# The softmax factors of a windowed attention, moved from VectorE to ScalarE

## The chip, the cores and the metric

The kernel runs on one core of one Trainium2 chip. The metric is the device time of the whole program in microseconds (us), median of several runs. The engines named below are TensorE (PE in the profile; its weight loads are PEld), VectorE (DVE), ScalarE (ACT), GpSimd (POOL) and SyncE (SP, which issues most DMAs).

## The reference, cut to what matters

The program computes two stacked transformer blocks: attention with a sink and a window, an MLP, a gated scan, a second MLP, and then a second model with attention, a state space layer and a mixture of experts. The change touches only the first attention, of 512 latent and 256 context tokens, with 16 heads of 64 in 4 groups that share keys:

```
def softmax_with_sink(s, sink):
    sk = sink.astype(jnp.float32)[None, :, :, None, None]
    m = jnp.maximum(jnp.max(s, axis=-1, keepdims=True), sk)
    e = jnp.exp(s - m)
    return e / (jnp.sum(e, axis=-1, keepdims=True) + jnp.exp(sk - m))
...
        p = softmax_with_sink(jnp.concatenate([s_lat, s_ctx], axis=-1), sink_g).astype(v.dtype)
        return (jnp.einsum('bhgqk,bkhd->bqhgd', p[..., :n_loc], v)
                + jnp.einsum('bhgqk,bkhd->bqhgd', p[..., n_loc:], v_ctx))
```

The kernel divides after the product with the values: it needs 1/(sum of the exponentials and the sink's term) for each query, which this text calls the factors.

## The kernel before, in words

All weights stream through a ring of four buffers. Each engine's program is written out by hand, in order, and semaphores tie the engines together; no planner reorders anything. So an instruction that waits holds up all that stands behind it on its engine.

The attention is 24 blocks (`WORK`, line 1019), numbered n: 4 groups of heads times 6 blocks of 128 queries, taken in the order b = 0, 1, 4, 2, 3, 5. Blocks 0 to 3 are latent and see their own key tile, the neighbours' and the two context tiles; blocks 4 and 5 are context and see the two context tiles alone. So the blocks of a group have 4, 5, 2, 5, 4 and 2 key tiles ("four-key", "five-key", "two-key" blocks below), 88 in all. Each key tile has 512 columns: 4 heads times 128 queries.

For block n TensorE does this in order (lines 1234 to 1248): for each key tile `key_scores` (lines 1209, 1212 and, at the window's edge, 1214) into one of two PSUM banks XP 0 and 1, where tile s waits until the exponential of tile s-2 has been taken; `turn_rows(n+1)` (line 1200), which waits for the sink's term of block n+1; a product that opens the output bank (line 1243); and for each key tile `weighted_values` (line 1221, each recorded as two products), which waits for the exponential of its tile. Among these stand the four `row_scores` of block n+2 (lines 1188 to 1194), whose first waits for `rows_low(n+1)` and whose third and fourth wait for VectorE's maxima of the first and second. VF holds ones beside the values, so rows 64 to 127 of the output bank (XP 2 + n % 2) are the sums, each of them in all 64 rows.

ScalarE for block n (line 1858 on): the exponential of each key tile (`exps`, line 1849), after the first of them `sink_term(n+1)` (line 1828); then `rows_high(n+1)` (1833), `queries_high(n+1)` (1841), and `mixed_high(n-1)` (1853), which waits for the divided output of block n-1.

VectorE for block n (line 2566 on): `normalise(n-1)`, `rows_low(n+1)` (line 2536), `mixed_low(n-1)` (line 2558), which waits for `mixed_high(n-1)`, and `maxima(n+2)` (four reductions in line 2521, then small steps in lines 2524 to 2531). `normalise` takes the factors in three steps, a transposition in 32 by 32 squares out of PSUM (line 2543), the reciprocal of the one column of each square that is needed (line 2545) and a transposition back of that column spread out (line 2547), and then multiplies the two halves of the output by them (line 2552).

After the last block come `normalise(23)`, `mixed_high(23)` and `mixed_low(23)`, and only then can TensorE begin the product with w_o (line 645).

Of the kernel before, what the change touches and what calls it, by code (L numbers as in the profile page):

```python
# [19 lines left out]
ACT = mybir.ActivationFunctionType  # L20
AX = mybir.AxisListType

P = 128
# [197 lines left out]
def backbone_kernel(nc, a, out_d):  # L221
# [19 lines left out]
    with ctx:  # L241
        sem_cache = {}

        def sem(name):
            if name not in sem_cache:
                sem_cache[name] = ctx.enter_context(nc.semaphore(name))
            return sem_cache[name]

        def sb(stack, name, shape, dt=F32):
            return stack.enter_context(nc.sbuf_tensor(name, shape, dt))  # L250
# [4 lines left out]
        with ExitStack() as s0:  # L255
            PT = sb(s0, "PT", [P, PT_RING, 512])
            QB = sb(s0, "QB", [P, 2, 4, P], FR)
            SPREAD = sb(s0, "SPREAD", [P, 4, P])
            RC = sb(s0, "RC", [P, 2, 2, P])
            RCT = sb(s0, "RCT", [64, 512])  # L260
            RCS = sb(s0, "RCS", [64, 16])
            OU = sb(s0, "OU", [P, 2, 2, P])

        with ExitStack() as s7:
# [280 lines left out]
        XP = ctx.enter_context(nc.psum_tensor("XP", [P, 4, 512], F32))  # L545
# [72 lines left out]
        def pieces(it, t, tokens):  # L618

            if it == 0 and t < 2:  # L620
                return [(2 * t + c, c, *halves_of(tokens)[t][0:2]) for c in range(2)]
            if tokens == T:
                return [(2 * t + c, t, 384 * c, 384 * c + 384) for c in range(2)]
            return [(t + 2, t, 0, LAT)]
# [396 lines left out]
        def values_through(n):  # L1021

            return WORK[n][5] + len(WORK[n][4])
# [702 lines left out]
        def _(act):  # L1726
# [98 lines left out]
            def sink_term(n):  # L1825

                act.wait_ge(sem("shift_spread"), 2 * n + 2)
                act.activation(SPREAD[:, :, 68:72], SINKS[:, :, :], ACT.Exp).then_inc(sem("sink_term"), 1)

            def rows_high(n):  # L1830

                act.wait_ge(sem("rows_turned"), n + 1)
                act.activation(QB[64:96, n % 2, :, :].rearrange("p (x c) n -> p x (c n)", x=2), DP[64:96, 1:4:2, 256:512], ACT.Copy
                               ).then_inc(sem("rows_high"), 1)

            def queries_high(n, g, b):

                if n >= 2:
                    act.wait_ge(sem("attended"), values_through(n - 2))
                for e in range(2):  # L1840
                    act.activation(QB[0:64, n % 2, 2 * e:2 * e + 2, :], A2[64 * e:64 * e + 64, e, 2 * g:2 * g + 2, b * P:(b + 1) * P].bitcast(F32),
                                   ACT.Copy).then_inc(sem("queries_copied"), 1)

            def exps(s):

                act.wait_ge(sem("keyed"), s + 1)
                if s >= PT_RING:
                    act.wait_ge(sem("attended"), s - PT_RING + 1)
                act.activation(PT[:, s % PT_RING, :], XP[:, s % 2, :], ACT.Exp).then_inc(sem("exponentials"), 1)

            def mixed_high(n, g, b):
                act.wait_ge(sem("normalised"), 2 * n + 2)
                act.activation(AH[:, 2 * g:2 * g + 2, b * P:(b + 1) * P], OU[:, n % 2, :, :], ACT.Copy).then_inc(sem("mixed_high"), 1)

            sink_term(0)
            rows_high(0)
            queries_high(0, 0, 0)
            for n, g, b, near, keys, first in WORK:
                for i in range(len(keys)):
                    exps(first + i)  # L1860
                    if i == 0 and n + 1 < len(WORK):
                        sink_term(n + 1)
                if n + 1 < len(WORK):
                    rows_high(n + 1)
                    queries_high(*WORK[n + 1][0:3])
                if n:
                    mixed_high(*WORK[n - 1][0:3])
            mixed_high(n, g, b)
            at.u += 32
            split_high(act, at, nxt)  # L1870
# [435 lines left out]
            for t in range(2):  # L2306
                split_high(act, at, nxt)
                for jj in range(2):
                    j = 2 * t + jj
# [93 lines left out]
        def _(dve):  # L2403
# [133 lines left out]

            def normalise(n):

                dve.wait_ge(sem("attended"), values_through(n))  # L2540
                bank_of = 2 + n % 2
                turned = RCT[:, :].rearrange("p (b n) -> p b n", n=32)
                dve.transpose(RCT[:, :], XP[64:P, bank_of, :]).then_inc(sem("denominators"), 1)
                dve.wait_ge(sem("denominators"), 3 * n + 1)
                dve.reciprocal(RCS[:, :], turned[:, :, 0:1].rearrange("p b n -> p (b n)")).then_inc(sem("denominators"), 1)
                dve.wait_ge(sem("denominators"), 3 * n + 2)
                dve.transpose(RC[0:64, :, :, :].rearrange("p e j n -> p (e j n)").rearrange("p (b n) -> p b n", n=32),
                              RCS[:, :].unsqueeze(2).to_broadcast((64, 16, 32))).then_inc(sem("denominators"), 1)
                dve.wait_ge(sem("denominators"), 3 * n + 3)
                out = XP[0:64, bank_of, :].rearrange("p (e j n) -> p e j n", e=2, j=2)  # L2550
                for e in range(2):
                    dve.tensor_tensor(OU[64 * e:64 * e + 64, n % 2, :, :], out[:, e, :, :], RC[0:64, e, :, :], ALU.mult
                                      ).then_inc(sem("normalised"), 1)
# [12 lines left out]
            for n, g, b, near, keys, first in WORK:  # L2566
                if n:
                    normalise(n - 1)
                if n + 1 < len(WORK):
                    rows_low(n + 1)  # L2570
                if n:
                    mixed_low(*WORK[n - 1][0:3])
                if n + 2 < len(WORK):
                    maxima(*WORK[n + 2][0:4])
            normalise(n)
            mixed_low(n, g, b)
            split_low(dve, nxt)
# [43 lines left out]
            for it in range(MLP_STEPS):  # L2621
# [14 lines left out]
                for t in range(2 * KT):  # L2636
# [5 lines left out]
                    for c in range(2):  # L2642
                        i = 2 * t + c
# [6 lines left out]
                        if t < KT:  # L2650
                            if i >= 2:
                                dve.wait_ge(sem("hidden_high"), it * 16 + (i - 1))
                            n = pieces(it, t, T)[c][3] - pieces(it, t, T)[c][2]
# [490 lines left out]
            for t in range(2):  # L3144
                split_low(dve, nxt)
                for jj in range(2):
                    j = 2 * t + jj
# [303 lines left out]
```

## Time and profile before

| what | us |
|---|---|
| median of 3 runs | 2658.0 (2656.53 to 2661.26) |
| the profiled execution | 2659.49 |
| its span | 2656.7 |
| TensorE busy in the span | 2461.1 |
| VectorE busy | 1693.7 |
| ScalarE busy | 1088.6 |

The profiled execution took 2.8 us more than its span, and 1.5 us more than the median. The attention's blocks run from about 206 to 409 us from the span's start. Shapes in rows are partitions by elements, and durations of single instructions include their latency, so neighbours on one engine may overlap a little.

### The profile page before, as it was taken

Reading aid. Unit: us, or ns where it says so; the run is one execution under the profiler, and the core shown is the slowest. Engines: PE = TensorE matmul, PEld = TensorE weight load, DVE = VectorE, ACT = ScalarE, POOL = GpSimd, SP = SyncE. Lnnn points to the kernel's source line nnn. Section 1 sums busy time; section 2 is a strip of 40 time slices with the busy share of each in tenths; the row PEclk is TensorE's granted clock in tenths of the full one; section 3 lists DMA queues with packets and bytes.
Section 4 is the critical chain, followed back from the end, with each engine's and each line's share of the span. In section 5 each row is a group of like instructions: output and inputs, shape, how many; then the busy total and the mean of one; then the engine's idle time right before and its main releaser. Section 6 shows DMA issues by size and latency. Waiting matters only on the chain. (4 is left out here: it accounts for less than half of the span.)

```text
span 2656.7 us, 32750 instructions
## 1 busy us (share of the span) xinstructions
PE 2461.1 (93%) x12252; PEld 2036.7 (77%) x12252; DVE 1693.7 (64%) x2746; ACT 1088.6 (41%) x1739; POOL 94.3 (4%) x111
## 2 busy tenths in 40 slices
PE   6968899899999999899998899998989999999999
PEld 5865558699999997687777688886766666777777
DVE  6666778765646466655553634445347997569986
ACT  4424443431313133423333422333446663377764
POOL 0000000000000000000000000000000330020000
PEclk8989999899999999889999999998999999999999
DMA  6220004133323232011111122222121221149995
GB/s 255 84 91 0 1 1 159 51 133 127 127 96 127 103 127 82 22 48 48 40 40 48 63 97 96 101 91 94 64 72 44 72 71 64 49 164 341 338 336 183
DMA packets 78131, 275.62 MB, mean 104 GB/s; under 512 B 8800, under 2 KB 9312, under 8 KB 77856
## 3 DMA queue, kind: packets, MB, share of 16 engines
q1 hardware_dynamic: 74016, 265.74, 28.5%
q10 hardware_dynamic: 3968, 7.88, 0.9%
q8 instruction: 97, 1.59, 0.2%
q14 instruction: 50, 0.41, 0.0%
HBM read 271.49 MB, written 2.10 MB: 103 GB/s over the span
## 5 line engine op out<-in xcount | busy, mean ns | idle before, releaser
L645 PE MATMUL DP<-HH,WL 128*128 128x384 f32 (+2 forms) x1408 | 517.7, 368 | 28.3 <-DVE WL L638 22.5
L646 PE MATMUL DP<-HH,WH 128*128 128x384 f32 (+2 forms) x1408 | 504.6, 358 | 0.0
L647 PE MATMUL DP<-HL,WH 128*128 128x384 f32 (+2 forms) x1408 | 504.5, 358 | 0.0
L638 DVE TENSOR_TENSOR WL<-RAW,WH 128x1024 fp32r<-128x1024 f32 x230 | 280.8, 1223 | 218.7 <-ACT WH L611 212.0
L645 PE MATMUL DP<-A,WL 128*128 128x384 f32 (+2 forms) x1072 | 381.7, 356 | 22.6 <-issue 8.4
L646 PE MATMUL DP<-A,WH 128*128 128x384 f32 (+2 forms) x1072 | 379.1, 354 | 0.0
L647 PE MATMUL DP<-A,WH 128*128 128x384 f32 (+2 forms) x1072 | 378.8, 353 | 0.0
L611 ACT ACTIVATE WH<-RAW 128x1024 fp32r<-128x1024 f32 x230 | 241.2, 1050 | 292.6 <-PE DP L647 205.0
L645 PEld LDWEIGHTS DP<-HH,WL 128*128 128x128 f32 x1408 | 267.5, 190 | 66.8 <-DVE WL L638 31.8
L646 PEld LDWEIGHTS DP<-HH,WH 128*128 128x128 f32 x1408 | 267.6, 190 | 29.2 <-issue 5.2
L647 PEld LDWEIGHTS DP<-HL,WH 128*128 128x128 f32 x1408 | 267.3, 190 | 25.5
L645 PEld LDWEIGHTS DP<-A,WL 128*128 128x128 f32 x1072 | 204.0, 190 | 43.1 <-issue 14.7
L775 DVE SCALAR_TENSOR_TENSOR MPROD<-RAW,COND 128x1024 f32<-128x1024 f32 x180 | 219.9, 1222 | 14.4 <-DMA RAW<-in_stream 7.1
L646 PEld LDWEIGHTS DP<-A,WH 128*128 128x128 f32 x1072 | 204.1, 190 | 16.6 <-issue 0.5
L647 PEld LDWEIGHTS DP<-A,WH 128*128 128x128 f32 x1072 | 204.0, 190 | 16.4
L3298 DVE TENSOR_TENSOR MW<-MRAW,MW 128x1024 fp32r<-128x1024 f32 x168 | 196.3, 1229 | 18.1 <-ACT MW L2352 17.8
L2352 ACT ACTIVATE MW<-MRAW 128x1024 fp32r<-128x1024 f32 x168 | 163.9, 1052 | 0.0
L645 PE MATMUL DP<-WH,HL 128*128 128x256 f32 x304 | 94.7, 311 | 18.5 <-issue 17.6
L2633 DVE TENSOR_TENSOR Y<-DP,Y 128x384 f32<-128x384 f32 (+2 forms) x64 | 35.1, 554 | 111.7 <-PE DP L647 111.7
L1920 ACT ACTIVATE SQ<-TQ 128x384 f32<-128x384 f32 (+2 forms) x64 | 33.6, 525 | 162.8 <-DVE TQ L2654 162.8
L645 PE MATMUL DP<-MW,G 128*128 128x512 f32 x224 | 89.4, 399 | 7.0 <-DVE MW L3298 6.9
L646 PE MATMUL DP<-WH,HH 128*128 128x256 f32 x304 | 92.0, 303 | 0.0
(419 smaller groups left out, 3863.7 us busy)
## 6 DMA issues: line engine op xcount, KB each, us to landing
RAW<-in_stream SPq DMA_DIRECT2D x326, 512.0 KB, 3.3
MRAW<-in_stream SPq DMA_DIRECT2D x168, 512.0 KB, 5.4
MATS<-in_ssm ACTq DMA_DIRECT2D x16, 256.0 KB, 2.6
X<-in_x SPq DMA_DIRECT2D x8, 384.0 KB, 10.0
BW<-in_rel ACTq DMA_DIRECT2D x4, 512.0 KB, 3.5
out<-X SPq DMA_DIRECT2D x8, 256.0 KB, 2.0
COND<-in_cond SPq DMA_DIRECT2D x1, 1024.0 KB, 4.9
CONST<-in_const SPq DMA_DIRECT2D x1, 256.0 KB, 4.9
```

The costliest lines, as they stand in the source:

```text
L611: act.activation(WH[:, nxt.d % WRING, :], RAW[:, nxt.u % RING, :], ACT.Copy).then_inc(hi_done, 1)
L638: dve.tensor_tensor(WL[:, w, :], RAW[:, nxt.u % RING, :], WH[:, w, :].bitcast(F32), ALU.subtract).then_inc(raw_done[nxt.u % RING], 1)
L645: pe.matmul(out, al, bh, start=first, stop=False)
L646: pe.matmul(out, ah, bh, start=False, stop=False)
L647: return pe.matmul(out, ah, bl, start=False, stop=last)
L775: dve.scalar_tensor_tensor(MPROD[:, :], RAW[:, at.u % RING, :], 1.0, COND[:, s, :], ALU.mult, ALU.mult, accum_out=MODT[:, col, s:s + 1]).t ...
L1920: act.activation(SQ[:, i % 2, 0:b0 - a0], r, ACT.Square)
L2352: act.activation(MW(i, 0)[:, t, :], MRAW[:, j % ERING, :], ACT.Copy).then_inc(hi_done, 1)
L2633: dve.tensor_tensor(y, DP[:, bank(at), 0:b0 - a0], y, ALU.add).then_inc(bank_free[bank(at)], 1)
L3298: dve.tensor_tensor(MW(i, 1)[:, t, :], MRAW[:, j % ERING, :], MW(i, 0)[:, t, :].bitcast(F32), ALU.subtract).then_inc(sem("expert_taken"), 1)
```

## The change

ScalarE makes the factors as exp(-ln(sum)), straight over the 64 rows of sums. A function `denominators(n-1)` with two activations is put into ScalarE's program of block n behind the first exponential and `sink_term(n+1)`, ahead of the second exponential; the one of the last block stands after the loop. VectorE's three steps and their buffers go, and `normalise` waits for ScalarE's two steps in their place.

```
             def mixed_high(n, g, b):
...
+            def denominators(n):
+
+                act.wait_ge(sem("attended"), values_through(n))
+                if n:
+                    act.wait_ge(sem("normalised"), 2 * n)
+                over = RC[0:64, :, :, :].rearrange("p e j n -> p (e j n)")
+                act.activation(over, XP[64:P, 2 + n % 2, :], ACT.Ln).then_inc(sem("denominators"), 1)
+                act.wait_ge(sem("denominators"), 2 * n + 1)
+                act.activation(over, over, ACT.Exp, scale=-1.0).then_inc(sem("denominators"), 1)
+
...
                     exps(first + i)
                     if i == 0 and n + 1 < len(WORK):
                         sink_term(n + 1)
+                    if i == 0 and n:
+                        denominators(n - 1)
...
                 if n:
                     mixed_high(*WORK[n - 1][0:3])
+            denominators(n)
             mixed_high(n, g, b)
...
             def normalise(n):
 
-                dve.wait_ge(sem("attended"), values_through(n))
                 bank_of = 2 + n % 2
-                turned = RCT[:, :].rearrange("p (b n) -> p b n", n=32)
-                dve.transpose(RCT[:, :], XP[64:P, bank_of, :]).then_inc(sem("denominators"), 1)
-                dve.wait_ge(sem("denominators"), 3 * n + 1)
-                dve.reciprocal(RCS[:, :], turned[:, :, 0:1].rearrange("p b n -> p (b n)")).then_inc(sem("denominators"), 1)
-                dve.wait_ge(sem("denominators"), 3 * n + 2)
-                dve.transpose(RC[0:64, :, :, :].rearrange("p e j n -> p (e j n)").rearrange("p (b n) -> p b n", n=32),
-                              RCS[:, :].unsqueeze(2).to_broadcast((64, 16, 32))).then_inc(sem("denominators"), 1)
-                dve.wait_ge(sem("denominators"), 3 * n + 3)
+                dve.wait_ge(sem("denominators"), 2 * n + 2)
```

## Rows read from the trace of the kernel before

**Rows 1.** Stretch: length, PE, PEld, DVE, ACT, POOL busy, granted clock, DMA share, GB/s.

```profile
206.00:409.00 203.00, 181.01 (x721) 109.25 (x720) 150.53 (x326) 95.39 (x205) 0.00 (x0) 1.00 0.00 1
225.00:233.00 8.00, 6.21 (x29) 3.90 (x28) 7.28 (x15) 3.13 (x7) 0.00 (x0) 1.00 0.01 3
```

**Rows 2.** Waits from 206 to 409: who waited for whom, total, times, longest.

```profile
PEld XP L1209 <- ACT PT L1849: 18.5, 32, 0.7
...
PE DP L1188 <- DVE QB L2536: 4.4, 7, 0.6
```

**Rows 3.** Groups by line, 206 to 412: busy, mean ns, idle before and its releaser.

```profile
L1849 ACT ACTIVATE PT<-XP 128x512 f32<-128x512 f32 x88 | 50.8, 593 | 99.1 <-PE XP L1212 54.8 <-PE XP L1214 44.3
...
L2543 DVE STREAM_TRANSPOSE RCT<-XP 64x512 f32<-64x512 f32 x24 | 17.2, 719 | 1.8 <-PE XP L1221 1.1
L2547 DVE STREAM_TRANSPOSE RC<-RCS 64x512 f32<-64x512 f32 x24 | 16.9, 703 | 0.8
...
L2545 DVE RECIPROCAL RCS<-RCT 64x16 f32<-64x16 f32 x24 | 5.9, 246 | 0.8
```

**Rows 4.** ScalarE's groups of the whole program, by shape.

```profile
L2170 ACT ACT_TABLE_LOAD x14 | 18.0, 1283 | 0.3
...
L2228 ACT ACTIVATE RS<-XP,EPSV 128x512 f32<-128x512 f32 x8 | 5.1, 692 | 8.9 <-PE XP L1525 8.9
...
L2232 ACT ACTIVATE RS<-RS 128x512 f32<-128x512 f32 x8 | 4.4, 620 | 0.0
```

**Rows 5.** Timeline of ScalarE outside the attention: start, duration, what.

```profile
49.68 0.90 ACT L855 ACTIVATE TR<-XP,EPSV 128x768 f32<-128x768 f32 x1
50.61 0.84 ACT L858 ACTIVATE TR<-TR 128x768 f32<-128x768 f32 x1
...
1115.50 0.62 ACT L1941 ACTIVATE QD<-BC 128x512 f32<-128x512 f32 x1
1116.02 0.62 ACT L1942 ACTIVATE KI<-BC 128x512 f32<-128x512 f32 x1
```

**Rows 6.** Timeline of a five-key block.

```profile
284.95 0.58 ACT L1849 ACTIVATE PT<-XP 128x512 f32<-128x512 f32 x1
...
285.77 0.39 PE L1209 MATMUL XP<-A,KDH 128*128 128x512 f32 x1
...
285.97 1.09 ACT L1849 ACTIVATE PT<-XP 128x512 f32<-128x512 f32 x2 [0.43 <-PE XP L1214]
...
286.62 0.50 PE L1209 MATMUL XP<-A,KDH 128*128 128x512 f32 x1 [0.23 <-ACT PT L1849]
```

**Rows 7.** Timeline of a four-key block.

```profile
294.11 0.59 ACT L1849 ACTIVATE PT<-XP 128x512 f32<-128x512 f32 x1
...
294.75 0.50 PE L1209 MATMUL XP<-A,KDH 128*128 128x512 f32 x1
```

**Rows 8.** Timeline of a two-key block.

```profile
277.49 0.72 DVE L2543 STREAM_TRANSPOSE RCT<-XP 64x512 f32<-64x512 f32 x1
...
277.61 0.58 ACT L1849 ACTIVATE PT<-XP 128x512 f32<-128x512 f32 x1
...
278.45 0.59 ACT L1833 ACTIVATE QB<-DP 32x512 fp32r<-32x512 f32 x1 [0.26 <-PE DP L1200]
...
279.26 0.87 DVE L2552 TENSOR_TENSOR OU<-XP,RC 64x256 f32<-64x256 f32 x2
280.16 0.69 DVE L2536 TENSOR_TENSOR QB<-DP,QB 32x512 fp32r<-32x512 f32 x1
...
281.00 0.35 PE L1188 MATMUL DP<-KDH,A 128*128 128x256 f32 x1 [0.63 <-DVE QB L2536]
...
281.62 2.69 DVE L2521 TENSOR_REDUCE TOP<-DP 128x1 f32<-128x512 f32 x4 [0.31 <-PE DP L1194]
```

**Rows 9.** Timeline of the last block.

```profile
403.82 0.19 PEld L1221 LDWEIGHTS XP<-PT,VF 128*128 128x128 f32 x1 [0.24 <-ACT PT L1849]
...
407.51 0.87 DVE L2552 TENSOR_TENSOR OU<-XP,RC 64x256 f32<-64x256 f32 x2
```

More of the change, by code:

```diff
@@ L259, in backbone_kernel @@
             RC = sb(s0, "RC", [P, 2, 2, P])
-            RCT = sb(s0, "RCT", [64, 512])
-            RCS = sb(s0, "RCS", [64, 16])
             OU = sb(s0, "OU", [P, 2, 2, P])
```

## The prediction

> **What bounds the kernel now.** I read the page's totals first: TensorE is busy 93% of the span, VectorE 64%, ScalarE 41%. That says nothing of the attention, so the second view is the busy time by stretch. In the 203 us of the 24 blocks TensorE is busy 181.0 us, VectorE 150.5, ScalarE 95.4, at a granted clock of 1.00 and without DMA traffic [rows 1]. TensorE is the fullest engine and has 22 us of gaps. The third view, the waits, says what ends them: most often a score product waits for an exponential (its weight load, 32 times, 18.5 us), and 7 times, in two-key blocks, the row scores wait for VectorE's `rows_low`, 4.4 us [rows 2]. ScalarE in turn idles 99 us ahead of exponentials [rows 3], but that idle time lies ahead of the first one of a block, while TensorE is at values and row scores. Within the key phase the two engines alternate over two PSUM banks, and there ScalarE has hardly a gap. The timelines of one block of each length [rows 6 to 8] show that, and on them the sum rests. The semaphores leave no other order: score tile s waits for exponential s-2.
>
> **What goes.** VectorE loses 24 transpositions of 719 ns, 24 reciprocals of 246 ns and 24 transpositions of 703 ns [rows 3], 40.0 us of busy time, and from the start of the first transposition to the first multiplication 279.26 - 277.49 = 1.77 us each time [rows 8]. What would be late next is the wait for ScalarE, worked out below.
>
> **What comes.** ScalarE gets 24 logarithms and 24 exponentials of 64x512. An exponential of 512 columns out of PSUM takes 0.58 to 0.60 us (593 ns mean) [rows 3, 6, 7], one from SBUF to SBUF 0.62 [rows 4, 5]. The only logarithms of 512 columns in the trace take 0.69 and read a bias from a tensor (EPSV) [rows 4]; the new one has none. So it costs between 0.58 and 0.69, and I take 0.60, by the exponential that also reads PSUM and has no bias operand. Half the partitions buy nothing: I keep the duration of 128, since no row of this shape speaks for less. The second must wait for the first; the same pair elsewhere shows 0.03 us between (49.68 + 0.90 = 50.58, then 50.61), and independent activations start 0.10 before the end of the one ahead (1115.50 + 0.62 against 1116.02) [rows 5]. The pair therefore moves the second exponential of a block by 0.60 + 0.03 + 0.62 - 0.10 = 1.15 us. Shortest: 1.10. Longest, with 0.69 and no overlap behind the pair: 1.34. The pair doesn't wait itself: the values of block n-1 are done before block n's keys, as TensorE goes in order, and so is `normalise(n-2)`. Queued behind it are the block's other exponentials, `rows_high`, `queries_high` and `mixed_high`.
>
> The Trainium skill ("ScalarE: Activation LUTs", section "What ACT_TABLE_LOAD costs") gives an activation with immediate scale and bias 186 ns + 0.833 ns per column, and some 93 ns more for each pointer operand; an estimate by it is 0.61 us for the logarithm, and the trace agrees in that the row with EPSV stands at 0.69. Were the bias handed over as a pointer after all, the pair would shift things by 1.24, and the sum below would be 14.4 in place of 13.1.
>
> **Five-key blocks (8).** The second exponential moves from 284.95 to 286.10 and ends at 286.68. The fourth score tile waits for it and starts 0.05 later, at 286.73 in place of 285.77 [rows 6]: 0.96 late. The third exponential follows in half a microsecond (two take 1.09), 286.60 to 287.19, where before it began at 285.97 because its scores weren't ready. So the fifth tile starts at 287.24 in place of 286.62: 0.62 late, a third of the shift being taken up by the gap of 0.43 that ScalarE had there. Nothing later in the block waits for slack: `turn_rows`, the values and the row scores follow in a chain on TensorE. 8 x 0.62 = 5.0. Bounds 0.57 and 0.80 (0.19 more with the longest pair): 4.6 and 6.4.
>
> **Four-key blocks (8, of which the first has no pair ahead).** The second exponential moves from 294.11 to 295.26 and ends at 295.85; the last score tile starts at 295.90 in place of 294.75 [rows 7], 1.15 late, with no gap behind it. 7 x 1.15 = 8.1; bounds 7.7 and 9.4.
>
> **Two-key blocks (7 without the last).** No score tile waits, but the second value product and the rest of ScalarE's queue do. From 277.61: logarithm to 278.21, exponential 278.24 to 278.86, the block's second exponential 278.76 to 279.34, `rows_high` from 279.26 in place of 278.45, to 279.85. VectorE multiplies from 278.90 (0.36 earlier than 279.26) to 279.77, so `rows_low` begins at 279.88 in place of 280.16, and the row scores at 280.72 in place of 281.00 [rows 8]: 0.28 early. TensorE's value products, moved by some 0.4, are still done by then, since it waited 0.63 there. But `queries_high` (0.85) and `mixed_high` (0.42) now end near 281.18 and `mixed_low` near 281.63, so the maxima start at 281.66, against 281.62: the gain is eaten, because the row scores wait for the maxima. In the other kind of two-key block, where the maxima began later, about 0.1 is kept. I take -0.2 for all 7; bounds -1.9 (0.28 each kept) and +1.1 (0.15 each, pair at its longest).
>
> **The end.** The second value product waits for the exponential that now comes 1.15 later [rows 9], and the last pair takes 1.25 with its start where the last transposition chain took 1.77, which had itself started half a microsecond after the values because of `mixed_low(22)`. The last multiplication then starts at 407.75 instead of 407.51: +0.2; bounds 0 and 0.5.
>
> **The sum.** 5.0 + 8.1 - 0.2 + 0.2 = 13.1 us; from the bounds 10.4 to 17.4. The profiled execution took 2659.5, so it becomes 2672.6. The median of the runs stood 1.5 below it at 2658.0, so I forecast a median of 2671.1 (2668.4 to 2675.4 by the bounds). Behind the attention all is moved as one: the weight ring stands full and no transfer runs [rows 1], so no stage after it gives time back. The 40 us that VectorE saves are worth nothing, as it then stands waiting for ScalarE.
>
> **The rivals.** *VectorE's chain sets the end, and ScalarE's pair hides in its idle time.* For it: ScalarE is idle more than half of the stretch, VectorE is at 7.28 of 8.00 us in a two-key block [rows 1], and the row scores wait for `rows_low`. Against it: the pair stands ahead of the second exponential by program order, and the idle time is elsewhere. It decides if ScalarE reaches the second exponential no later than TensorE needs it. Then the 4.4 us of waits [rows 2] go and 0.5 at the end: 2658.0 - 4.9 = 2653.1. Chance 0.05.
>
> *The stalls are partly made good*, because a later wait of the same block (for the maxima, the sink's term) was long enough to take them, so that only four-key blocks lose, about half: 2658 + 4 = 2662. Against it: those waits follow TensorE's own products by a fixed chain and move with them. Chance 0.07.
>
> *The pair costs more than its two durations*: the whole of ScalarE's tail comes late in two-key blocks as well, row scores start late in place of early, 0.5 each, and the pair is at its longest: 6.4 + 9.4 + 3.5 + 0.5 = 19.8, 2677.8. Chance 0.10.
>
> *Tables are switched.* If logarithm and exponential needed their own tables, 48 loads of 1283 ns [rows 4] would add 61.6 us: some 2733. Against it: the pair at 49.68 and 50.61 runs with no load between [rows 5]. The Trainium skill (same page, section "Table sets: the hidden batching unit") says that one set holds both functions; I found none of its loads within the attention. Chance 0.02. The forecast keeps 0.76.
>
> **How the numbers follow.** A difference under 0.2%, 5.3 us, can't be told from none here. Faster by more: nearly only the first rival's upper part, 0.04. Within: the rest of it and most of the second, 0.07. Slower: 0.89. The range for 8 in 10 takes in the bounds of the sum and reaches toward the second and third rivals: 2664 to 2679.
>
> **What would show it.** ScalarE's second exponential starts some 1.15 later after the first one in each block but block 0; the waits of L1209 for L1849 grow by some 13 us; the fourth tile of a five-key block and the last of a four-key block carry them; the multiplication starts 0.3 earlier in relation to the sink's term; the maxima in two-key blocks stay where they were; the attention's stretch takes 216 us, at clock 1.00, and no stage behind it changes its length. TensorE stood at 78% busy in 225 to 233 at a granted clock of 1.00 [rows 1], so 84% over the stretch should not lower it. A lower clock there, a table load, a logarithm over 0.7 us, or key phases that don't lengthen would prove the forecast wrong.

## The result, and the profile after

The changed kernel takes 2680.1 us in the median (2678.4 to 2686.3, 4 runs) against 2659.6 (2656.5 to 2662.2, 4 runs): ratio 1.0082, 95% interval 1.0067 to 1.0096. A second set of 5 runs gave 1.0083 (1.0069 to 1.0097). It is 20.5 us slower; the forecast had 13.1, and its range ended at 2679.0.

The busy time by stretch of the kernel after (columns as in [rows 1]), the attention's whole length. It begins 4.9 us later here, so the stretch is laid as in [rows 1], from 1.1 us ahead of the first exponential:

```profile
210.90:435.70 224.80, 186.52 (x721) 109.79 (x720) 110.47 (x254) 126.06 (x253) 0.00 (x0) 0.98 0.00 1
```

The stretch is 21.8 us longer. VectorE's busy time falls by 40 us and ScalarE's rises by 31, TensorE's work is the same 721 matmuls, and the mean clock is no longer 1.00: the granted clock is 0.50 up to 3.0 us behind the first exponential, and once more from 327.6 to 331.0 us. The waits of the same kernel, 211 to 436 us, answer to [rows 2]:

```profile
DVE OU L2555 <- ACT RC L1861: 40.3, 24, 3.5
...
PEld XP L1207 <- ACT PT L1847: 36.5, 39, 2.1
PE XP L1207 <- ACT PT L1847: 21.5, 27, 1.7
...
PE DP L1186 <- DVE QB L2547: 2.1, 7, 0.3
```

The loads of score products waited 18.5 us for exponentials before and wait 36.5 now. What VectorE saved it spends waiting for the factors: 40.3 us. The groups by line show the pair itself, the logarithm (L1859) and its exponential (L1861):

```profile
L1861 ACT ACTIVATE RC<-RC 64x512 f32<-64x512 f32 x24 | 15.1, 630 | 0.8
...
L1859 ACT ACTIVATE RC<-XP 64x512 f32<-64x512 f32 x24 | 14.3, 595 | 1.1 <-PE XP L1219 0.5
```

595 and 630 ns, against 600 and 620 taken: the durations were right. The timeline of a five-key block after, for [rows 6]:

```profile
296.61 0.60 ACT L1847 ACTIVATE PT<-XP 128x512 f32<-128x512 f32 x1 [3.18 <-PE XP L1212]
...
297.13 0.22 ACT L1826 ACTIVATE SPREAD<-SINKS 128x16 f32<-128x16 f32 x1
...
297.37 0.60 ACT L1859 ACTIVATE RC<-XP 64x512 f32<-64x512 f32 x1
...
298.00 0.63 ACT L1861 ACTIVATE RC<-RC 64x512 f32<-64x512 f32 x1
298.66 1.09 ACT L1847 ACTIVATE PT<-XP 128x512 f32<-128x512 f32 x2
298.66 0.87 DVE L2555 TENSOR_TENSOR OU<-XP,RC 64x256 f32<-64x256 f32 x2 [1.57 <-ACT RC L1861]
299.31 0.50 PE L1207 MATMUL XP<-A,KDH 128*128 128x512 f32 x1 [1.08 <-ACT PT L1847]
```

The second exponential starts 2.05 behind the first. Before it was 0.63, from this start to 284.95 [rows 6]:

```profile
284.32 0.60 ACT L1849 ACTIVATE PT<-XP 128x512 f32<-128x512 f32 x1 [3.74 <-PE XP L1214]
```

So it moved by 1.42, not by 1.15, and at the pair's three joints nothing overlaps: each instruction starts 0.02 to 0.03 behind the end of the one ahead. A four-key block after, for [rows 7]; its last score tile starts 2.66 behind the first exponential, before it was 294.75 - 293.51 = 1.24. The first line is that of the kernel before:

```profile
293.51 0.60 ACT L1849 ACTIVATE PT<-XP 128x512 f32<-128x512 f32 x1 [3.59 <-PE XP L1214]
```

```profile
306.69 0.60 ACT L1847 ACTIVATE PT<-XP 128x512 f32<-128x512 f32 x1 [3.59 <-PE XP L1212]
...
309.35 0.50 PE L1207 MATMUL XP<-A,KDH 128*128 128x512 f32 x1 [1.28 <-ACT PT L1847]
```

A two-key block, for [rows 8]: the first exponential before, then the block after:

```profile
276.62 0.60 ACT L1849 ACTIVATE PT<-XP 128x512 f32<-128x512 f32 x1 [4.96 <-PE XP L1212]
```

```profile
288.49 0.60 ACT L1847 ACTIVATE PT<-XP 128x512 f32<-128x512 f32 x1 [4.97 <-PE XP L1210]
...
291.52 0.59 ACT L1831 ACTIVATE QB<-DP 32x512 fp32r<-32x512 f32 x1
...
292.14 0.69 DVE L2547 TENSOR_TENSOR QB<-DP,QB 32x512 fp32r<-32x512 f32 x1 [0.37 <-ACT QB L1831]
292.97 0.36 PE L1186 MATMUL DP<-KDH,A 128*128 128x256 f32 x1 [0.30 <-DVE QB L2547]
293.01 0.42 ACT L1851 ACTIVATE A<-OU 128x256 fp32r<-128x256 f32 x1
...
293.46 0.43 DVE L2561 TENSOR_TENSOR A<-OU,A 128x256 fp32r<-128x256 f32 x1 [0.63 <-ACT A L1851]
...
293.92 2.69 DVE L2532 TENSOR_REDUCE TOP<-DP 128x1 f32<-128x512 f32 x4
```

`rows_low` starts 3.65 behind the first exponential (before 3.54), the maxima 5.43 (before 5.00): they wait behind `mixed_low`, that for `mixed_high`, and that stands at the end of ScalarE's late queue.

Block lengths, from one first exponential to the next, are the measure below. After less before, in all 23 intervals: four-key +1.40 to +1.44 (six of them), five-key +0.81 to +0.97, two-key +0.42 and +0.25 in turn; besides, +0.75 in block 0, which has no pair, and +3.06 in block 12.

### The profile page after: what moved, and what is told of

Read it like the earlier page. It is cut to its first block and busy times, and to the rows that moved or that the text cites. A ratio compares the mean times of both kernels' runs of the same rounds, so it can differ in the third digit from the quotient of the medians.

```text
span 2684.5 us, 32749 instructions
## 1 busy us (share of the span) xinstructions
PE 2473.8 (92%) x12252; PEld 2042.4 (76%) x12252; DVE 1653.9 (62%) x2674; ACT 1119.6 (42%) x1787; POOL 94.3 (4%) x111
```

## The experiments

**The same kernel again.** No edit.

> The changed kernel once more, unedited, to see how much of its profile was the change and how much the spread of an execution. Its first profile had 4.9 us more than the kernel before ahead of the attention and a stretch of half clock in one four-key block. If these belong to the execution and not to the change (my theory), the attention from its first exponential to its last block's is 215.0 to 216.2 us long here, in place of 217.4, the blocks of 4, 5 and 2 key tiles are longer than before by 1.42, 0.88 and 0.24 to 0.42 us as in the first profile, and the median stands 19 to 21 us over the kernel before. If the change itself costs time outside the attention (rival), the stretch ahead of it is again some 5 us longer and the median 24 us or more over.

2680.5 us, ratio 1.0083 (1.0069 to 1.0097). The first exponential is at 207.38 (before 207.08; the first profile 211.98), so the 4.9 us ahead of the attention belonged to that execution. The attention is 217.41 long, before 195.55: the expected shortening didn't come, since block 12 has its +3.07 here too. The timeline of TensorE there and, under it, the busy time by stretch of this run:

```profile
320.92 0.40 PE L1210 MATMUL XP<-QB,KDL 128*128 128x512 f32 x1
322.98 0.78 PE L1207 MATMUL XP<-A,KDH 128*128 128x512 f32 x1 [1.67 <-ACT PT L1847]
323.56 0.63 PE L1210 MATMUL XP<-QB,KDL 128*128 128x512 f32 x1
```

```profile
322.00:323.00 1.00, 0.02 (x1) 0.02 (x1) 0.63 (x2) 0.98 (x3) 0.00 (x0) 1.00 0.00 0
323.00:324.00 1.00, 1.00 (x3) 0.70 (x4) 0.21 (x1) 0.42 (x1) 0.00 (x0) 0.52 0.00 0
324.00:325.00 1.00, 1.00 (x6) 1.00 (x5) 0.00 (x0) 0.60 (x1) 0.00 (x0) 0.50 0.00 0
...
326.00:327.00 1.00, 1.00 (x3) 0.53 (x2) 0.39 (x1) 0.94 (x3) 0.00 (x0) 0.78 0.00 0
327.00:328.00 1.00, 1.00 (x4) 0.50 (x3) 0.53 (x2) 0.00 (x0) 0.00 (x0) 1.00 0.00 0
```

TensorE stood idle for 1.67 us waiting for the delayed exponential, and its granted clock then was 0.50, the 1.2 GHz level, for some 3.5 us (the same product takes 0.63 in place of 0.40). That is a cost of the change: 3.07 - 1.42 = 1.65 us.

**The pair alone, on top of the kernel before.** VectorE unchanged, nobody waits for the pair.

```
+            def pair(n):
+                act.wait_ge(sem("attended"), values_through(n))
+                over = RC2[0:64, :, :, :].rearrange("p e j n -> p (e j n)")
+                act.activation(over, ONES[64:P, 0:1].to_broadcast((64, 512)), ACT.Ln).then_inc(sem("pair"), 1)
+                act.wait_ge(sem("pair"), 2 * n + 1)
+                act.activation(over, over, ACT.Exp, scale=-1.0).then_inc(sem("pair"), 1)
...
                     if i == 0 and n + 1 < len(WORK):
                         sink_term(n + 1)
+                    if i == 0 and n:
+                        pair(n - 1)
```

> The kernel before, with only ScalarE's logarithm and exponential put in behind the first exponential and the sink's term of each block, on a spare buffer and with a constant of ones in SBUF as the input (out of PSUM it would read the bank that VectorE reads); nobody waits for them, VectorE keeps its transpositions. Theory A (the pair's place in ScalarE's order is the whole cost, by delaying the second exponential by some 1.45 us): 17 to 21 us slower than before, the last score tile of a four-key block 1.4 late. Rival B (the cost is VectorE's new wait for the factors, with multiplication and rows_low behind it): 0 to 5 us slower, because that wait is absent here.

2679.2 us, ratio 1.0073 (1.0058 to 1.0089), 19.7 slower. Theory A stands, rival B falls: with VectorE as it was, nearly the whole loss is there. Four-key blocks +1.30, five-key +0.76, two-key +0.31 and +0.16. They are each 0.09 to 0.14 less than in the changed kernel (block 6, with 1.7 us more behind a fall of the clock, and block 0 left out), and its ScalarE shows why:

```profile
300.14 0.22 ACT L1829 ACTIVATE SPREAD<-SINKS 128x16 f32<-128x16 f32 x1
300.38 0.63 ACT L1860 ACTIVATE RC<-CONST 64x512 f32<-64x512 f32 x1
301.04 0.63 ACT L1862 ACTIVATE RC<-RC 64x512 f32<-64x512 f32 x1
301.58 1.06 ACT L1850 ACTIVATE PT<-XP 128x512 f32<-128x512 f32 x2
```

Here the second exponential starts 0.09 ahead of the pair's end (301.67), as the prediction had assumed.

**VectorE's steps gone, nothing in their place.** The output is multiplied by a constant; the division is left out.

```
-                dve.transpose(RCT[:, :], XP[64:P, bank_of, :]).then_inc(sem("denominators"), 1)
...
-                dve.wait_ge(sem("denominators"), 3 * n + 3)
...
+            dve.memset(RC[0:64, :, :, :], 0.01)
```

> The kernel before without VectorE's three steps and with nothing in their place: the output is multiplied by a constant, so the division by the sums is left out. Theory A (VectorE's chain binds only in the two-key blocks and at the end): rows_low there starts 1.1 earlier, TensorE is at most 0.6 earlier per two-key block, 8 x 0.6 = 4.8, and 1.8 at the end: 5 to 7 us faster than before. Rival B (VectorE's 40 us bind nothing): 0 to 1. Rival C (they bind throughout): over 15 faster.

2647.4 us, ratio 0.9956 (0.9940 to 0.9971), 12.2 faster. In the trace, two-key blocks are 0.76 and 0.86 shorter, four- and five-key blocks 0.00 (block 0 apart), and the way from the last block's first exponential to the first w_o product is 6.29 in place of 8.50. So VectorE's chain binds where theory A has it, with 0.8 per block in place of 0.6. This accounts for 5.9 + 2.2 = 8.1 us, and the interval of the time begins at 8. The other 4 us of the median are found nowhere in the trace: the profiled execution, the slowest of the four, took 3.8 us more than the kernel before behind the first w_o product.

**The pair ahead of the first exponential.**

```
+                if n:
+                    denominators(n - 1)
                 for i in range(len(keys)):
                     exps(first + i)
                     if i == 0 and n + 1 < len(WORK):
                         sink_term(n + 1)
-                    if i == 0 and n:
-                        denominators(n - 1)
```

> The changed kernel with the pair moved ahead of the block's first exponential, where ScalarE idles 2.7 to 5.0 us. Theory A: the second exponential goes back to 0.63 behind the first in long blocks; the first is late only where the values of the block before ended under 1.3 us ahead of it: some 0.3 to 0.5 in the four four-key blocks behind a five-key block and in the two-key blocks (where it hides), 0.1 elsewhere. In two-key blocks VectorE multiplies 1.8 earlier, rows_low 1.1 earlier, TensorE 0.6 earlier. Together -4.8 + 2.3 - 0.5 = -3 against before, 22 to 24 faster than the changed kernel. Rival B (ScalarE's extra work or the wait for factors costs wherever it stands): 10 or more slower than before.

2655.2 us, ratio to the kernel before 0.9980 (0.9964 to 0.9995): 4.4 faster than before, 25 faster than the changed kernel with the same instructions. Rival B falls. ScalarE in a two-key block of this run:

```profile
301.81 0.60 ACT L1859 ACTIVATE RC<-XP 64x512 f32<-64x512 f32 x1 [2.26 <-PE XP L1219]
302.43 0.63 ACT L1861 ACTIVATE RC<-RC 64x512 f32<-64x512 f32 x1
303.09 0.60 ACT L1847 ACTIVATE PT<-XP 128x512 f32<-128x512 f32 x1
...
304.09 0.58 ACT L1847 ACTIVATE PT<-XP 128x512 f32<-128x512 f32 x1
```

The pair now lies in idle time that waited for the values, and the second exponential is 1.00 behind the first, as before (302.60 - 301.49 = 1.11). Two-key blocks are 1.06 and 0.98 shorter than before. The long blocks lose 0.1 to 0.5 each (block 22 loses 0.8, block 0 has no pair), since `attended` comes little more than a microsecond ahead of the first scores there and the pair makes the first exponential late. In the trace the attention is only 0.7 us shorter than before, 194.8 in place of 195.6, of which block 0 alone took 1.1 more, and the way to the first w_o product 0.9 shorter: 1.7 us. The rest of the 4.4 isn't located; the interval is 1.3 to 9.6 us.

**Both ways side by side.** The pair only ahead of two-key blocks and for the last output, VectorE's steps elsewhere.

```
+        ON_ACT = [n - 1 for n in range(1, len(WORK)) if len(WORK[n][4]) == 2] + [len(WORK) - 1]
...
             for n, g, b, near, keys, first in WORK:
+                if n - 1 in ON_ACT:
+                    factors(n - 1)
                 for i in range(len(keys)):
                     exps(first + i)
...
+                if n in ON_ACT:
+                    dve.wait_ge(sem("factors"), 2 * ON_ACT.index(n) + 2)
+                else:
...
+                    dve.transpose(RCT[:, :], XP[64:P, bank_of, :]).then_inc(sem("denominators"), 1)
```

> Both ways side by side: in the eight two-key blocks (and for the last block's output) ScalarE's pair, ahead of the first exponential; in all other blocks VectorE's transpositions and reciprocal as before. Theory A (a pair ahead of the first exponential costs only where the block before left it under 1.3 us, and gains only in two-key blocks, where VectorE's chain binds): from the blocks of pair_first, +0.29 - 1.06 + 0 + 0.1 - 0.98 + 0 per group of six, four groups, and -0.9 at the end: 7 to 8 us faster than before, 3 faster than pair_first. Rival B (pair_first's gain came from VectorE's freed time in all blocks): no faster than pair_first, since 16 blocks get VectorE's work back.

2652.1 us, ratio to the kernel before 0.9984 (0.9972 to 0.9996): 5.4 faster than before in medians. It is the lowest median of the kernels that compute all factors. Blocks per group: +0.29, -1.06, +0.01, +0.12, -0.98, +0.01, as summed up in advance. Even so the 7 to 8 us expected didn't come: the trace has 4.1 in the blocks and 0.9 at the end. The sum in advance counted the last two-key block twice, as a block and in the end's 0.9, and it had no loss for block 22 (+0.83, since no row scores stand there between its values and the keys of the last block) nor for block 0 (+0.69). Its lead over the pair ahead of every block isn't settled by the times: they were measured against different sets of the kernel before, and the intervals overlap. The traces have it: the attention is 191.45 long here, 194.83 there.

**The second activation left out.** The factors aren't computed; the output is multiplied by the logarithm.

```
-                act.wait_ge(sem("denominators"), 2 * n + 1)
-                act.activation(over, over, ACT.Exp, scale=-1.0).then_inc(sem("denominators"), 1)
...
-                dve.wait_ge(sem("denominators"), 2 * n + 2)
+                dve.wait_ge(sem("denominators"), n + 1)
```

> The changed kernel without the second activation of the pair: the output is multiplied by the logarithm of the sum, so the factors aren't computed. Theory A (the delay of the second exponential counts, minus the gap that stood behind it): the delay falls from 1.42 to 0.76; four-key blocks are 0.76 longer than before in place of 1.42, five-key blocks some 0.2 in place of 0.88, two-key blocks about as before; 5 to 8 us slower than before, and no stretch of half clock inside the attention, since TensorE's longest gap falls to 1.0. Rival B (a fixed cost of the hand-over from ScalarE to VectorE): 14 or more slower.

2660.5 us, ratio 1.0012 (1.0001 to 1.0023), 3 slower, less than the 5 to 8 expected; the trace has 5.7 more in the blocks and 1.2 less at the end. Four-key blocks +0.75, five-key +0.22: both as expected, which shows the gap of five-key blocks at work. Two-key blocks -0.24 and -0.41 where 0 was expected, and no half clock inside the attention. So 0.66 less delay brings two-key blocks 0.66 each: they have no slack for it at all.

**What keeps ScalarE's instructions from overlapping.** Three kernels, one execution of each. First the pair's exponential over 128 rows, then the logarithm written to the rows where it is read:

```
-                act.activation(over, over, ACT.Exp, scale=-1.0).then_inc(sem("denominators"), 1)
+                whole = RC[:, :, :, :].rearrange("p e j n -> p (e j n)")
+                act.activation(whole, whole, ACT.Exp, scale=-1.0).then_inc(sem("denominators"), 1)
```

> The changed kernel with the pair's exponential over all 128 rows of its buffer (the lower 64 hold numbers that nobody reads). The block's second exponential started 0.03 behind its end in the changed kernel, where the prediction had it 0.10 ahead of that end. If the change of rows from 64 to 128 is what keeps neighbours from overlapping: it now starts 0.1 ahead of the end, some 2 us faster than the changed kernel in all. If it isn't (pair_added, whose pair covered the same 64 rows and did overlap, speaks for that): 0.03 behind as before, and the time is unchanged.

```
-                act.activation(over, XP[64:P, 2 + n % 2, :], ACT.Ln).then_inc(sem("denominators"), 1)
+                below = RC[64:P, :, :, :].rearrange("p e j n -> p (e j n)")
+                act.activation(below, XP[64:P, 2 + n % 2, :], ACT.Ln).then_inc(sem("denominators"), 1)
```

> The changed kernel with the logarithm written to rows 64 to 127, where it is read, and the exponential taking it from there to rows 0 to 63. If the shift from rows 64 to 127 down to 0 to 63 costs the logarithm its overlap with the sink's term (0.24 from start to start, in place of 0.12): 0.12 now, and the shift's cost moves to the exponential, which has to wait for the logarithm anyway; some 2.5 us faster. If not: unchanged starts, unchanged time. The joint behind the exponential says the same as in exp_whole.

2679.0 and 2677.6 us. In both, the starts around the pair are where they were in the changed kernel (0.24 from the sink's term to the logarithm, 0.03 behind the pair). Neither the number of rows of the exponential nor the logarithm's shift to other rows is the cause. Then the logarithm's source:

```
-                act.activation(over, XP[64:P, 2 + n % 2, :], ACT.Ln).then_inc(sem("denominators"), 1)
+                act.activation(over, ONES[64:P, 0:1].to_broadcast((64, 512)), ACT.Ln).then_inc(sem("denominators"), 1)
```

> The changed kernel with the logarithm's input taken from a constant of ones in SBUF in place of the sums in PSUM, so the division is left out; everything else, VectorE's wait for the factors too, stays. In the changed kernel the block's second exponential starts 0.03 behind the end of the pair's, in pair_added 0.09 ahead of it, and these kernels differ in two things there. If the logarithm's source is what counts: the second exponential starts 0.09 ahead here. If it is that VectorE waits for the pair (its multiplication starts at that moment): 0.03 behind, as in the changed kernel. Time 0 to 3 us under the changed kernel either way.

2674.4 us, and the timeline has the overlap back, 292.76 against an end at 292.86:

```profile
291.32 0.22 ACT L1826 ACTIVATE SPREAD<-SINKS 128x16 f32<-128x16 f32 x1
291.56 0.63 ACT L1859 ACTIVATE RC<-CONST 64x512 f32<-64x512 f32 x1
292.23 0.63 ACT L1861 ACTIVATE RC<-RC 64x512 f32<-64x512 f32 x1
292.76 1.06 ACT L1847 ACTIVATE PT<-XP 128x512 f32<-128x512 f32 x2
```

So it is the source of the logarithm, and not VectorE's wait: in all 23 blocks with a pair the exponential behind it starts 0.02 to 0.03 behind its end in the changed kernel and 0.09 to 0.10 ahead of it here. The source was changed in two things at once, SBUF in place of PSUM and one column spread out in place of 512 columns; which of them counts was not tested. Nor does reading PSUM prevent an overlap by itself: two exponentials out of PSUM side by side take 1.09 us, at 0.60 each.

This kernel also settles what VectorE's steps are worth. It differs from the pair alone in its buffer and in that VectorE has no transpositions and waits for the pair. Their blocks agree within 0.03 us (block 0 and those with a fall of the clock left out); only the end is 0.5 us shorter. The other lost overlap, sink's term to logarithm, is in all of these runs and stays open; in the kernel before, the two copies of `queries_high`, whose inputs begin at rows 0 and 64, don't overlap either (0.42 each, 0.86 for both), which would fit a cost of changing the first row, but that was not tested by itself.

## Why the prediction was wrong

| term | forecast | measured (same kernel again, blocks) |
|---|---|---|
| five-key blocks, 8 | +5.0 | +7.1 |
| four-key blocks, 7 | +8.1 | +9.9 |
| two-key blocks, 7 | -0.2 | +2.4 |
| the end | +0.2 | +0.1 |
| clock at half behind a gap (block 12) | 0 | +1.65 |
| sum | +13.1 | +21.2 |

The medians have 20.5. Block 0's +0.76, which has no pair in it, is left out: it lay between -0.28 and +1.08 in the other kernels. The granted clock was still 0.50 there for 0.5 us behind the first exponential in the kernel before, and for 3.0 us in the changed one. Single executions also differ outside the attention, by 2242 to 2249 us behind the first w_o product, so the sum and the medians agree only within some microseconds.

- *The mechanism was right.* The pair's place ahead of the second exponential is the cost (the pair alone +19.7, ahead of the first exponential -4.4), it falls on the tiles named, and behind it VectorE's 40 us are worth nothing, as forecast, but for 0.5 us at the end. Without the pair they would be worth 8: the steps left out gained 0.8 in each two-key block and 2.2 at the end. One reading was too broad: of the 99 us for which ScalarE idles ahead of exponentials, 8.5 lie within the key phases, among them the 0.43 that the sum for five-key blocks rightly used.
- *The step that failed is the size of the shift*, "0.60 + 0.03 + 0.62 - 0.10 = 1.15". Measured: 1.42. The durations held. The missing 0.27 are in the main two overlaps that the sum took for granted, 0.12 ahead of the logarithm (against the exponential that had stood in its place) and 0.13 behind the pair; the pair itself took 0.01 more. The longest value, 1.34, was still too short. In four-key blocks 0.27 comes out in full (1.15 forecast, 1.42 measured), in five-key blocks nearly so (0.62 and 0.88). Over the 22 blocks it makes some 6 of the 8.1 us that the sum was short.
- *The two-key term had the wrong sign.* The chain was right, from the second exponential through `rows_high`, `queries_high`, `mixed_high` and `mixed_low` to the maxima. But it took the 0.27, and 0.10 more because `rows_high` doesn't overlap the exponential ahead either (291.52, behind its end at 291.49; in the kernel before its timeline shows the same in long blocks, 288.01 behind 287.98). The maxima start 0.43 late in place of 0.04. The leave-out run shows it one for one.
- *That "84% over the stretch should not lower" the clock* was wrong. The row at 78% with clock 1.00 was an average over short gaps. What came before the fall was one idle stretch of 1.67 us. Of the kernels run, those with gaps of 1.55 to 1.68 us in four-key blocks (the changed one, again, the pair alone, and the three kernels on overlaps) had one or two falls inside the attention, at 1.65 each, though not behind every such gap (three in each kernel), and one of them stood behind a gap of 1.27. Where the gaps inside the attention stayed at 1.0 or less there was none. What makes one gap count and the next not was not found.
- *The first rival* (the pair hides in ScalarE's idle time) became true as soon as the pair stood in that idle time. The third rival's 2677.8, forecast at 0.10, was the nearest case: pair longer than its durations, whole tail late.
- *The tables* weren't switched: no load in the attention.

## What to carry to other kernels

When work moves to an engine that is idle half of the time, look where in its program order the idle time lies: the same two instructions cost 20 us behind the first exponential and gained some 2 (by the trace) to 4 (by the medians) ahead of it. In a chain of short instructions, count the overlaps between neighbours and take them as lost unless rows show the same pair of neighbours overlapping; two of little more than a tenth of a microsecond made nearly a fifth of the shift here. A sum of stalls can have a second price: behind some gaps of 1.3 to 1.7 us, and behind none of 1.0 or less, TensorE's clock fell here, at 1.65 us each.

## What the runs showed of the hardware that was not expected

An activation behind a pair whose first instruction read PSUM (64x512) started 0.03 us after the pair's end; with the same instruction reading one spread-out column of SBUF it started 0.10 before that end, each in all 23 blocks with a pair. The Trainium skill ("ScalarE: Activation LUTs", section "What ACT_TABLE_LOAD costs") says that back-to-back activations overlap by some 93 ns: the rows from 1115.50 on [rows 5] agree, the changed kernel's five-key block does not at any of its three joints around the pair, one of which is a wait on the instruction ahead. And a gap of 1.67 us in TensorE's work was followed by some 3.5 us at the granted clock 0.50, in block 12 in both profiles of the changed kernel and in the one with the exponential over 128 rows, while two equal gaps in each of these traces were not.
